# The even mixer's latent units: the place of the probabilities' eviction on ACT, of the logits and of the values on PE

## The reference, cut to what matters

```python
def block(args):
    i, ql, qi, wi, qb, fq = args
    ...
    _, sel = lax.top_k(score, k_sel)                      # 128 keys per query
    la = einsum('bthr,btkr->bhtk', ql, c_sel) + bias      # 8 latent heads, rank 128
    pa = softmax(where(valid, la, -inf))
    oa = einsum('bhtk,btkr->bthr', pa, c_sel)
    lb = einsum('bthd,bshd->bhts', qb, k_b) + fq - cum_f  # 8 forgetting heads, width 64
    pb = softmax(where(causal, lb, -inf))
    ob = einsum('bhts,bshd->bthd', pb, v_b)
o_a = einsum('bshr,hrd->bshd', oa, w_uv)
return concat([o_a, o_b]) @ w_o
```

## Time and profile before

| what | value |
|---|---|
| median of three runs | 2199.35 us (2198.8 to 2199.62) |
| span of the profiled execution | 2196.9 us |
| time of the profiled execution itself | not listed apart from its span |
| PE, DVE, ACT, POOL busy over the span | 94%, 56%, 41%, 13% |
| latent units, first logits to last half of values | 225.1 to 303.9 us |
| PE busy from 225.1 to 307.5 us | 65.9 of 82.4 us |

### The profile page before, as it was taken

The page is one execution under the profiler, slowest core; times in us unless marked ns, Lnnn a source line. Parts: engine busy times, 40 slices in busy tenths (PEclk is TensorE's granted clock), DMA queues, the critical chain, the costliest instruction groups (busy, mean ns, idle before and its releaser), DMA issues. The chain is left out here.

```text
span 2196.9 us, 26996 instructions
## 1 busy us (share of the span) xinstructions
PE 2061.2 (94%) x9546; PEld 1632.9 (74%) x9546; DVE 1237.6 (56%) x1910; ACT 908.6 (41%) x1403; POOL 288.2 (13%) x380
## 2 busy tenths in 40 slices
PE   8999889999999999999999988888887998999997
PEld 6666556888888677688888857877765676888886
DVE  3666447788677656755664444666546544333333
ACT  4333535444422443444442255566447534222222
POOL 0032401001000010000000013666410001000000
PEclk9999999999999999999999999999998999999999
DMA  5511012566444322222333212011110022332321
GB/s 170 146 46 39 1 48 98 172 193 196 149 159 158 100 85 79 77 88 97 97 107 106 90 46 68 30 39 39 58 39 1 1 87 75 98 95 95 115 92 51
DMA packets 52779, 193.93 MB, mean 88 GB/s; under 512 B 5808, under 2 KB 8528, under 8 KB 52312
## 3 DMA queue, kind: packets, MB, share of 16 engines
q1 hardware_dynamic: 44824, 165.18, 23.7%
q0 software_dynamic: 7344, 27.27, 3.9%
q10 hardware_dynamic: 528, 0.40, 0.1%
HBM read 189.15 MB, written 3.68 MB: 88 GB/s over the span
## 5 line engine op out<-in xcount | busy, mean ns | idle before, releaser
L196 PE MATMUL psum<-xH,w_hi 128*128 128x512 f32 x1800 | 728.2, 405 | 41.2 <-DVE xL L1372 20.6
L196 PE MATMUL psum<-xL,w_hi 128*128 128x512 f32 x1800 | 711.4, 395 | 0.0
L196 PE MATMUL psum<-xH,w_lo 128*128 128x512 f32 x1800 | 711.0, 395 | 0.0
L166 DVE TENSOR_TENSOR w_lo<-w_raw,w_hi 128x1024 fp32r<-128x1024 f32 (+1 forms) x273 | 356.9, 1307 | 365.4 <-ACT w_hi L160 365.0
L160 ACT ACTIVATE w_hi<-w_raw 128x1024 fp32r<-128x1024 f32 (+1 forms) x273 | 303.3, 1111 | 416.6 <-PE psum L196 407.4
L196 PEld LDWEIGHTS psum<-xH,w_hi 128*128 128x128 f32 x1800 | 344.0, 191 | 140.0 <-DVE xL L1372 36.1
L196 PEld LDWEIGHTS psum<-xH,w_lo 128*128 128x128 f32 x1800 | 344.0, 191 | 73.9
L196 PEld LDWEIGHTS psum<-xL,w_hi 128*128 128x128 f32 x1800 | 344.4, 191 | 71.0 <-issue 3.1
L196 PE MATMUL psum<-hidH,w_hi 128*128 128x512 f32 x528 | 206.2, 391 | 0.0
L196 PE MATMUL psum<-hidH,w_lo 128*128 128x512 f32 x528 | 205.4, 389 | 0.0
L196 PE MATMUL psum<-hidL,w_hi 128*128 128x512 f32 x528 | 205.4, 389 | 0.0
(11 more groups left out here) (321 smaller groups left out, 2497.1 us busy)
## 6 DMA issues: line engine op xcount, KB each, us to landing
w_raw<-in_up SPq DMA_DIRECT2D x132, 512.0 KB, 3.5
w_raw<-in_down SPq DMA_DIRECT2D x48, 704.0 KB, 4.1
mod_raw<-in_mod POOLq DMA_DIRECT2D x48, 512.0 KB, 3.9
w_raw<-in_sb_in SPq DMA_DIRECT2D x26, 512.0 KB, 3.5
w_raw<-in_ev_in SPq DMA_DIRECT2D x23, 512.0 KB, 3.7
w_raw<-in_od_in SPq DMA_DIRECT2D x20, 512.0 KB, 3.5
w_raw<-in_ev_out SPq DMA_DIRECT2D x8, 512.0 KB, 3.6
w_raw<-in_od_out SPq DMA_DIRECT2D x8, 512.0 KB, 3.5
```

Of the source, the lines that this page charges most:

```text
L166: nc.vector.tensor_tensor(w_lo[:, s % SPLIT, 0:w.cols], raw[:, s, 0:w.cols], w_hi[:, s % SPLIT, 0:w.cols].bitcast(F32), ALU.subtract).then ...
L196: mm = nc.tensor.matmul(acc, a[:, slot % SPLIT, cut], b[:, k0 + k, :], start=start and n == 0, stop=stop and n == 2)
```

## The change

Nothing is added to or taken from the work. In the latent part ACT's step evicts the probabilities of s - 4 ahead of the exponential of s (for the forgetting heads it stays behind). PE's step 32 makes the logits of 32 and 33, each later one those of s + 1, so that they are one unit ahead; and values_a at k = 1 stands behind the turn, no longer ahead of the logits.

```diff
@@ ACT
                 def step(s):
+                    latent = s >= UNITS
+                    if latent and s < len(units) + OUT:
+                        prob_out(s - OUT)
                     if s < len(units):
                         i = units[s][1]
                         act.wait_ge(a["ttr"], s + 1)
                         t = tl[:, s % RING, 0:(i + 1) * P]
                         nc.scalar.activation(t, t, ACT.Exp, ...)
-                    if OUT <= s < len(units) + OUT:
+                    if not latent and s >= OUT:
                         prob_out(s - OUT)
@@ PE
                 def step(s):
                     i, k = (s - UNITS) // HEADS, (s - UNITS) % HEADS
-                    if s >= UNITS and i and k == 1:
-                        values_a(i - 1, 0)
-                    if s < len(units):
+                    if s <= UNITS:
                         logits(s)
+                    if UNITS <= s < len(units) - 1:
+                        logits(s + 1)
                     if TURN <= s < len(units) + TURN:
                         turn(s - TURN)
                     if PV <= s < UNITS + PV:
                         values_b(s - PV)
                     if s >= UNITS:
+                        if i and k == 1:
+                            values_a(i - 1, 0)
                         if i + 1 < NB and k in (0, 3):
                             queries(i + 1, k // 3)
```

## The result

The changed kernel takes 2182.23 us (median of four runs, 2179.94 to 2186.65) against 2199.07 for the kernel before: 16.8 us less. The ratio, taken over the runs of both, is 0.9925 with a 95% interval of 0.9911 to 0.9939, which is 13.4 to 19.6 us. The forecast was 2184.0, between 2180.1 and 2193.

The account below looks back on a forecast made before the run. A ring of waits, no full engine, bounds the latent stage; with PE's work as the bound it ends 14.4 us earlier, the tail gives 0.9: 2196.9 - 15.3 + 2.45 = 2184.0 us, range 2180.1 to 2193.

Parts of the forecast that it names:

- ring of waits: Latent rows: each second unit goes round DVE scores, ACT exponential, ACT eviction, PE turn, PE logits, DVE; no engine is full.
- Part 1: ACT evicts unit s-4 ahead of the exponential of s; the turn then waits for DVE's normalise, about 277.7 instead of 278.53.
- new wait: On ACT, the exponential of s stands behind PE's turn of s-4; price 0 to 20 us, taken as 0.
- Part 2: PE issues logits one unit ahead and values behind the turn; PE's own work should become the bound, values no longer starving DVE.
- The sum: PE's work from first latent logits to values of row 3: 51.0 us, 52.9 with hand-overs and stalls, 54.9 with the unseen.
- hand-overs: 0.1 us at each query group in the latent rows, 0.6 us in all.
- two stalls: About 0.5 us at k = 0 of row 1 behind L749, and 0.8 at the end where values wait for L755.
- the unseen: Whether already met waits cost PE something, as idle weight loads at L837 suggest; bounds 0 and 4.6 us, taken as 2.0.
- The tail: Last values to values of the latent block: 5.0 us from start to start instead of 5.87, 0.9 less.
- Rival 1: PE stays tied to DVE's normalise at the turns; 6 us gained, 2193; chance 0.14.
- Rivals 3 and 4: 3: outputs-to-values chain sets the pace, no gain, 2199, chance 0.06; 4: exponential behind the turn slows it, 2205, chance 0.06.
- Rival 2: DVE and POOL exclude each other, four rows taking 58.9 us; 7.0 us gained and 0.9 in the tail, 2191.5; chance 0.12.

Follow-up runs that it names:

- Part 1 alone: Only ACT's eviction of s-4 ahead of the exponential of s for latent units, PE's order unchanged, against the kernel before: 2192.7 us, ratio 0.997.

## Why the prediction was right, point by point

- *The bound is a ring of waits.* Shown: 17.2 us of added PE work cost 10.0 us before and 16.8 after, and 9.5 us of added ACT work cost 5.3 us of time before (at least 3.2 of stage) and 0.3 of stage after.
- *Part 1 alone leaves the turn waiting for the normalise.* Shown, at L848. The changed kernel would lose little without this part: 0.85 us of stage. I had costed its new wait at 0, and ACT's waits for turns (L599, 1.9 and 2.2 us in all) are indeed harmless.
- *Part 2 makes PE the bound.* Shown; it alone brings 15.1 of 15.9 us. The logits carry 12.9 of these, the values' place 2.2 on top of them, 1.0 of it in the tail. One sentence of mine was wrong: that values no longer starve DVE. It still waits 21.1 us for logits, up to 2.5 at a time. PE does not wait for what follows from it.
- *The sum.* From first logits to values of row 3 are 54.35 us (279.49 - 225.14) against my 54.9. That it fits so well is in part luck, since two errors offset each other. I had 51.0 us for PE's products and 3.9 for hand-overs, two stalls and the unseen. Taken from start to start in the trace, the products are 53.7: logits 18.7 (mine 17.2), turns 10.9 (9.3), values 10.3, queries 6.5, forgetting values 4.2 (4.6), outputs 3.1. PE is idle for 0.65 us in two places: 0.24 at a turn at 237.38 that waits for a normalise, and 0.41 at the last turn, which waits for an eviction; values follow it without waiting for the low part. So the 1.9 us for hand-overs and stalls were 0.65, and the 2.0 for the unseen were 2.7. They lie in logits and turns, which I had scaled down from 512 columns; narrow ones cost more than their share, as one logits product of 128 columns with the turn behind it shows, 0.33 us instead of 0.215:

```profile
229.40 0.49 PE L840 MATMUL psum<-ev_hT,qlT 128*128 128x128 f32 x2
229.73 0.60 PE L848 MATMUL psum<-ident,logits 128*128 128x128 f32 x4
```

- *The tail.* 4.87 us against my 5.0.
- *The gain,* 15.9 us of stage against 15.3.
- *The time.* 2184.0 forecast, 2182.23 measured. The span cancels in my sum, which is the earlier median less the gain, 2199.35 - 15.3. From 2199.35 to 2182.23 are 17.1 us, 15.9 of them in the stage. The other 1.2 are not explained by the change; the four runs' own spread is 6.7 us, and the profiled execution gained only 11.9 us of span (2196.9 to 2185.0). That the median is off by less than 2 us is therefore luck in part.
- *The rivals.* Rival 1 holds for part 1 alone. Rivals 3 and 4 did not come: in the rows PE never waits for the low part, and DVE's reciprocal never for an exponential. Rival 2 (DVE and POOL exclude each other) I judged by half of the evidence. The Trainium skill (SBUF — State Buffer, "Who interferes with whom") says that where DVE is in a 2-port mode, the first of the two to issue gets the shared ports and the other waits for all of it. The earlier trace rows had DVE's normalise first, and I read POOL's start inside it as overlap. Where POOL's tensor_tensor is first, DVE's wait is plain. Timeline of the changed kernel, DVE and POOL:

```profile
245.20 0.35 DVE L746 TENSOR_SCALAR logits<-logits,stat 128x256 f32<-128x256 f32 x1
...
245.76 0.72 POOL L507 TENSOR_TENSOR addend<-score,near_bias 128x256 f32<-128x256 f32 x1
...
245.87 0.77 DVE L746 TENSOR_SCALAR logits<-logits,stat 128x256 f32<-128x256 f32 x1
```

At 245.20 the normalise of 256 columns takes 0.35 us; at 245.87, 0.11 us behind POOL's start, it takes 0.77 and ends 0.16 us after POOL (246.48). That is in line with the rule, though the trace does not show the whole 0.35 us behind POOL's recorded end. With DVE first the wait hides in POOL's record. Timeline of the kernel before, twice a normalise and the same addend of 128 columns:

```profile
257.74 0.35 DVE L743 TENSOR_SCALAR logits<-logits,stat 128x256 f32<-128x256 f32 x1
257.92 0.40 POOL L504 TENSOR_SCALAR addend<-score,far_bias 128x128 f32<-128x128 f32 x1 [3.53 <-DVE stat L736]
...
260.55 0.42 DVE L743 TENSOR_SCALAR logits<-logits,stat 128x384 f32<-128x384 f32 x1
260.74 0.47 POOL L504 TENSOR_SCALAR addend<-score,far_bias 128x128 f32<-128x128 f32 x1 [0.58 <-DVE stat L736]
```

POOL's equal work is 0.07 us longer behind a normalise that is 0.07 longer, and ends 0.23 and 0.24 us after it. So the earlier trace rows do not speak against the rule, as I had said. The rival's price did not come, though: the four rows took 51.4 us, less than DVE's 31.2 and POOL's 27.7 together, so the two did not exclude each other throughout. DVE's busy time in the rows was 31.3 before, and DVE is not the bound.

## What to carry to other kernels

When engines that share a hand-written order wait in turn, look for the ring and count over how many units it closes: giving the front of the pipeline one more unit of stock brought 12.9 us where taking one station out of the ring brought 4.8 to 6.5. Set long instructions (here the values) behind as much issued stock as the buffers allow. Then add a known amount of work to one engine in both versions: what it costs says which engine is on the path. Waits alone did not: DVE still waited 21 us for logits when PE had become the bound. Look at the clock of each run before its time is read.

## What the hardware showed besides

The granted clock fell to its lower level (0.50, 1.2 GHz) for short stretches. Most of them lie at the same distance behind the stage in the profiles of both kernels, and some come in one execution and not in another. In the changed kernel's profile one such stretch lies right behind the stage; table of stretches:

```profile
290.00:292.00 2.00, 0.35 (x2) 0.34 (x3) 1.04 (x2) 0.45 (x1) 0.00 (x0) 1.00 0.00 0
292.00:294.00 2.00, 2.00 (x8) 1.55 (x7) 0.62 (x2) 0.00 (x0) 0.00 (x0) 0.65 0.46 154
294.00:296.00 2.00, 2.00 (x6) 1.62 (x5) 0.00 (x0) 0.00 (x0) 0.00 (x0) 0.50 0.92 371
296.00:298.00 2.00, 2.00 (x10) 1.58 (x9) 0.00 (x0) 0.00 (x0) 0.00 (x0) 1.00 0.02 8
```

PE had been busy for 0.35 of the 2 us ahead of it, behind a tail with idle times of 0.83, 0.69 and 1.84 us. The products there took 0.63 us instead of 0.39. The profile of the kernel before has none at this place, though its tail has idle times of 1.32, 0.69 and 1.84 us. The changed kernel's four runs had mean clocks of 0.977, 0.977, 0.984 and 0.983 and took 2186.65, 2182.98, 2181.49 and 2179.94 us. The two with the lower clock are the longer ones, but they differ by 3.7 us from each other, so the clock is at best a part of the spread. In the profiled executions the part behind the stage was 4.0 us longer in the changed kernel, and some 5 us more of it were at the lower level (counted in steps of 2 us: 95.6 against 90.5), which can have cost 2.6 us at most; the rest is open. Differences of a few microseconds are therefore read here from the stage's length, and that only where its clock is 1.00. What sets the place of such a stretch stays open.
